# Expert weights in 4 MB loads over two neighbouring slots of a ring

## The reference: what is computed

```
for each block of tokens of expert e:
    gu = xb @ w_gate_up[e] + b_gate_up[e]        # (1024 x 2048) weights, 8 MB
    gate, up = split(gu); gate = min(gate, 7); up = clip(up, -7, 7)
    hmid = (up + 1.0) * (gate * sigmoid(1.702 * gate))
    out = hmid @ w_down[e] + b_down[e]           # (1024 x 1024) weights, 4 MB
y[token] += gate_weight * out
```

## Time and profile before

| what | value |
|---|---|
| time, median of 3 runs | 1261.79 us (1261.73 to 1263.7) |
| span of the profiled execution | 1260.1 us |
| TensorE matmul busy | 1172.9 us (93%) |
| TensorE weight load busy | 505.3 us (40%) |
| VectorE busy | 304.5 us (24%) |
| ScalarE busy | 205.2 us (16%) |
| SyncE's data queue: share of 16 engines | 83.1%, 439.30 MB |

### The profile page before, as it was taken

One profiled execution on the slowest core, in us unless ns is written; L12 is line 12 of the kernel. 1 busy time (PEld: TensorE's weight loads), 2 busy tenths in 40 slices (PEclk: granted clock), 3 DMA queues, 4 the chain that ended last, 5 costly groups with the idle time before them and its releaser, 6 DMA issues.

```text
span 1260.1 us, 17850 instructions
## 1 busy us (share of the span) xinstructions
PE 1172.9 (93%) x6963; PEld 505.3 (40%) x6963; DVE 304.5 (24%) x728; ACT 205.2 (16%) x384; POOL 3.1 (0%) x7
## 2 busy tenths in 40 slices
PE   7999999999899999999999888899999999999895
PEld 3476644685433333333333333333333333333332
DVE  3336463234702111112111111112111112111112
ACT  2120254132201111111111111111111111111111
POOL 0000000000000000000000000000000000000000
PEclk9998899999889999999999999999999999999999
DMA  9710064531889999999999999999999999999993
GB/s 366 322 67 2 2 266 148 219 134 67 347 360 429 426 429 426 428 427 427 428 426 428 428 428 428 427 428 429 427 428 427 429 426 428 427 428 428 428 427 143
DMA packets 37215, 440.48 MB, mean 350 GB/s; under 512 B 5536, under 2 KB 5664, under 8 KB 11456
## 3 DMA queue, kind: packets, MB, share of 16 engines
q1 hardware_dynamic: 36144, 439.30, 83.1%
q10 hardware_dynamic: 1008, 0.21, 0.1%
HBM read 438.45 MB, written 1.05 MB: 349 GB/s over the span
## 4 chain that ended last, share of the span: by engine, by line
PE 64%; DMA 21%; DVE 10%; issue 2%; ACT 2%; DVEq 1%; SPq 0%; ACTq 0%
PE bank L1355 24%; DMA ring<-in_w_gate_up 20%; PE bank L1376 15%; PE bank L1040 4%; PE bank L1070 2%; PE bank L1062 2%; PE bank L1226 2%; PE bank L1217 2%; PE bank L1282 2%; DVE work L914 2%; DVE work L999 2%; DVE work L995 1%; PE bank L1367 1%; DVE work L996 1%; ACT work L580 1%
## 5 line engine op out<-in xcount | busy, mean ns | idle before, releaser
L1355 PE MATMUL bank<-ring,work 128*64 128x512 f32 x2112 | 465.9, 596 | 23.6 <-DMA ring<-in_w_gate_up 23.6
L1355 PEld LDWEIGHTS bank<-ring,work 128*64 128x64 f32 x2112 | 146.8, 137 | 324.3 <-issue 270.8
L1376 PE MATMUL bank<-ring,work 128*64 128x512 f32 x1056 | 233.9, 595 | 22.6 <-ACT work L580 22.6
L1376 PEld LDWEIGHTS bank<-ring,work 128*64 128x64 f32 x1056 | 72.9, 137 | 162.4 <-issue 131.9
L995 DVE TENSOR_SCALAR work<-bank 128x512 f32<-128x512 f32 x33 | 22.8, 692 | 323.1 <-PE bank L1355 323.1
L577 ACT ACTIVATE work<-work 128x512 f32<-128x512 f32 x33 | 20.8, 630 | 472.4 <-DVE work L995 472.4
L909 DVE CAST work<-cst 96x64 bf16 (+1 forms) x34 | 6.5, 191 | 334.7 <-PE bank L1355 334.7
L1336 PE MATMUL bank<-work 64*128 64x512 f32 x272 | 67.6, 615 | 0.7 <-ACT work L586 0.7
L1327 PEld LDWEIGHTS bank<-work 128*128 128x128 bf16 x1632 | 50.6, 99 | 29.1 <-issue 28.3
L1040 PE MATMUL bank<-ring,work 128*128 128x488 f32 x128 | 54.4, 589 | 8.2 <-DMA ring<-in_w_in 8.2
L584 ACT ACTIVATE work<-bank 128x512 f32<-128x512 f32 x33 | 19.7, 597 | 237.2 <-PE bank L1376 237.2
(11 more groups left out here) (232 smaller groups left out, 765.8 us busy)
## 6 DMA issues: line engine op xcount, KB each, us to landing
ring<-in_w_gate_up SPq DMA_DIRECT2D x128, 2048.0 KB, 32.0
ring<-in_w_down SPq DMA_DIRECT2D x64, 2048.0 KB, 31.4
ring<-in_w_mkv SPq DMA_DIRECT2D x8, 1024.0 KB, 23.5
ring<-in_w_in SPq DMA_DIRECT2D x8, 976.0 KB, 17.0
ring<-in_w_o SPq DMA_DIRECT2D x1, 4096.0 KB, 13.1
ring<-in_w_mq SPq DMA_DIRECT2D x1, 4096.0 KB, 24.1
ring<-in_w_mo SPq DMA_DIRECT2D x1, 4096.0 KB, 12.9
work<-in_xT SPq DMA_DIRECT2D x2, 512.0 KB, 8.0
```

Source lines behind the costliest of these rows:

```text
L1355: ins = mm(bank[n // 2][lo:lo + BLK, :], xgT[:, k * BLK:(k + 1) * BLK], up_rows(j, k)[:, n * 512:(n + 1) * 512], start=False, stop=(k == K ...
L1376: ins = mm(bank[3][n * BLK:(n + 1) * BLK, :], lhs, down_rows(j, f)[:, n * 512:(n + 1) * 512], start=(f == 0), stop=(f == KC - 1))
```

## The change

From chunk 10 on, the loads go out in pairs: one transfer of 4 MB fills two neighbouring slots, 32 KB in a row per partition, both in HBM (the arrays are now laid out with two chunks of an expert per partition run) and in SBUF (the seventh and eighth places of `REGION` are swapped, so that each even slot and the next one are neighbours). It waits until the second of the two old chunks has been used for the last time, and both slots' readers wait for the one semaphore of the even slot. The first ten chunks are still loaded one by one, each now as half of a 32 KB run in HBM, and chunks 6 and 7 change places in the order. TensorE still uses and frees chunk by chunk.

```diff
-REGION = (2, 3, 4, 5, 8, 9, 7, 6, 0, 1)
+REGION = (2, 3, 4, 5, 8, 9, 6, 7, 0, 1)
...
+        def slot_pair(j):
+            return ring[:, REGION[j % NSLOT] * SLOT:(REGION[j % NSLOT] + 2) * SLOT]
...
             def load_chunk(j):
                 e, c = divmod(j, NCH)
-                src = wgu[c, :, e, :] if c < NGU else wdn[c - NGU, :, e, :]
-                sp.dma_start(slot(j), src).then_inc(ld_slot[j % NSLOT], 16)
+                src = wgu[c // 2, :, e, :] if c < NGU else wdn[0, :, e, :]
+                sp.dma_start(slot(j), src[:, c % 2 * SLOT:(c % 2 + 1) * SLOT]).then_inc(ld_slot[j % NSLOT], 16)
...
-            load_chunk(6)
+            load_chunk(7)
             sp.wait_ge(S["wm_mm"], 4)
             load_chunk(8)
             load_chunk(9)
             sp.wait_ge(S["rt_mm"], 2)
-            load_chunk(7)
+            load_chunk(6)
...
             def load_next(j, e, lasts):
+
                 c = j % NCH
-                back, freed = (2, c + NCH - NGU) if c < NGU else (1, c - NGU)
+                back, freed = (2, c + 1 + NCH - NGU) if c < NGU else (1, c + 1 - NGU)
                 sp.wait_ge(S["chunks_used"], lasts[2 - back] * NCH + (freed + 1))
-                src = wgu[c, :, bass.ds(e, 1), :] if c < NGU else wdn[c - NGU, :, bass.ds(e, 1), :]
-                sp.dma_start(slot(j), src).then_inc(ld_slot[j % NSLOT], 16)
+                src = wgu[c // 2, :, bass.ds(e, 1), :] if c < NGU else wdn[0, :, bass.ds(e, 1), :]
+                sp.dma_start(slot_pair(j), src).then_inc(ld_slot[j % NSLOT], 16)
...
-            for c in range(NGU, NCH):
-                load_next(NCH + c, 1, (first, first))
+            load_next(NCH + NGU, 1, (first, first))
...
-                    for c in range(NCH):
+                    for c in range(0, NCH, 2):
                         load_next((LEAD + r) * NCH + c, e, lasts)
...
+            def chunk_in(j):
+                if j < NSLOT:
+                    pe.wait_ge(ld_slot[j], 16)
+                else:
+                    pe.wait_ge(ld_slot[j % NSLOT // 2 * 2], (j // NSLOT + 1) * 16)
...
                     if k % ROWS == 0:
-                        pe.wait_ge(ld_slot[(j + k // ROWS) % NSLOT], ((j + k // ROWS) // NSLOT + 1) * 16)
+                        chunk_in(j + k // ROWS)
...
                     if f % (2 * ROWS) == 0:
-                        d = j + NGU + f // (2 * ROWS)
-                        pe.wait_ge(ld_slot[d % NSLOT], (d // NSLOT + 1) * 16)
+                        chunk_in(j + NGU + f // (2 * ROWS))
...
-        "w_router": w_router[0], "b_router": b_router[0], "w_gate_up": by_partition(w_gate_up[0], NGU),
-        "b_gate_up": b_gate_up[0], "w_down": by_partition(w_down[0], NDN), "b_down": b_down[0], "g_final": g_final,
+        "w_router": w_router[0], "b_router": b_router[0], "w_gate_up": by_partition(w_gate_up[0], NGU // 2),
+        "b_gate_up": b_gate_up[0], "w_down": by_partition(w_down[0], NDN // 2), "b_down": b_down[0], "g_final": g_final,
```

## The result

| | before | after |
|---|---|---|
| median | 1262.82 us (1261.73 to 1263.7, 8 runs) | 1265.45 us (1263.86 to 1267.33, 8 runs) |
| span of the profiled execution | 1260.1 us | 1261.9 us |

The ratio is 1.0022, 95% interval 1.0013 to 1.0031: slower by 2.6 us in the medians, between 1.6 and 3.9 us by the interval. Forecast were +1.3 us, 1263.1, and a range of 1257.0 to 1267.8. The profiled execution after, with 1263.86 us, was the fastest of its eight; its span is only 1.8 us above that of before.

The account below looks back on a forecast made before the run. The end was taken as set by the unbroken load stream from chunk 16, plus TensorE's work after the last g3. Start +3.42, tail +3.44, streaming -5.6 gave +1.3 us: 1263.1 us, range 1257.0 to 1267.8.

Parts of the forecast that it names:

- the forecast case: Whole kernel: streaming saves 3 to 9 us and no new gap opens, 1259.7 to 1265.7 us; chance 0.50.
- three signs named for a wrong forecast: Profile after: rate unmoved or moved over 1%, idle DMA engines in a window after 372, or clock below 1.00 after 400.
- rival C: Waits merged into one of 2.4 us lower TensorE's clock; in the last item +2.1 us, 1265.2; chance 0.10.
- D: Load queue runs dry at (20, 21) or the two-item expert: +1 to +3 us, to 1266; chance 0.08.
- Start, +3.4: Start of unbroken stream: pair (16, 17) waits for chunk 17's condition, going out at 371.99 instead of 368.57, +3.4 us.
- Streaming, -5.6: Load stream from (16, 17): 32 KB runs save fixed cost a = 8 ns, 64 ns per pair, 87 pairs, -5.6 us.
- A: Load stream: longer runs save as much again per byte, 11.8 us, net -4.9, 1256.9 us; chance 0.17.
- B: Load stream: 32 KB runs move as two of 16 KB or gain nothing; +6.9, 1268.7 us; chance 0.15.
- The 7.9 us lost on the way: Stream from chunk 16 to last g3: 1222.7 worked out, 1230.56 seen; instruction packets would account for it, carried over unchanged.
- Tail, +3.44: After the last gate-up landing: g2 and g3 land together, so 16 more matmuls follow, +3.44 us.
- No gap at (20, 21): Early stream: pair (20, 21) goes out in time, 393.6 against 394.1, margin 0.5 us, so no gap.
- The expert with two items, 0 with +0.5: Load at the two-item expert: gap of 0.4 us at most, hidden by slower engines; taken as 0, keeping +0.5.

Follow-up runs that it names:

- the run with chunk 16 alone: Changed kernel with only the pair (16, 17) loaded one by one; 1264.05 us, 1.0013 against the kernel before.
- the run of the tail: Changed kernel with only g2 and g3 of the last expert loaded one by one; 1262.52 us, 0.9995 against the kernel before.
- the run with added matmuls in the last two experts: Changed kernel with 8 zero-adding matmul instructions before the wait for g2 in experts 30 and 31; 1264.01 us, 1.0011 against the kernel before.
- long-run experiments: Changed kernel with pairs and waits kept but the old HBM layout, two 16 KB runs per partition; 1270.11 us, 1.0047 against the kernel before.

## Why the prediction was right, and where its sizes were off

The forecast of +1.3 us lies 0.5 below what the profiled execution shows and 1.3 below the medians. The mechanism held, but that the sum came so near is in part luck: the stream gained 0.8 us more than forecast, and 1.2 us more were lost on the way. Of the three signs named for a wrong forecast two came true: a window after 372 shows idle DMA engines (0.04 from 902 to 904), and the granted clock fell below 1.00 after 400. The third did not, as the rate moved by 0.7%. So what happened is the forecast case with a small share of rivals C and D in it.

- **What bounds the kernel**: right. The end follows the unbroken stream of loads from chunk 16 on. The runs that undo the start and the tail move the end by about the amounts worked out (2.8 and 3.4 us, together 5.3, and 6.1 with the last three experts one by one); each of these has an interval of more than 1 us on either side.
- **Start, +3.4**: measured 3.42 in the trace; 2.8 came back when it was undone, with seven pairs (0.5 us) less of the faster stream.
- **Streaming, -5.6**: 87 pairs x 73 ns = -6.4. A run of 32 KB costs 9.713 / 8 = 1214 ns, 9 ns less than two of 611.6; a was 9, not 8. Neither limit (nothing, 11.8 us) came near, so rivals A and B were both wrong. The packets went from 37215 to 24110 [page of either kernel]. Two runs made one in 91 pairs are 91 x 128 packets less, and 91 transfers less are 91 x 16 small ones: 13104 of the 13105. A cut into pieces of 16 KB would not give that.
- **The 7.9 us lost on the way, carried over**: the forecast put them down to packets of instructions. The completions show where they are: the first engine finished the last g3 at 1222.0, as the sum without loss gives (1222.7), the last one at 1230.5. So it is the drift of the engines; that the packets cause it is not shown.
- **Tail, +3.44**: 3.4 measured from the last wait to the end.
- **No gap at (20, 21)**: right, with the margin as small as said: in the run with chunk 16 alone, 3.4 us less of queue opened it.
- **The expert with two items, 0 with +0.5**: the reasoning was that slower engines would hide the gap. They did where the clock stayed (0.0 us at the landing in the run of the tail) and hid all but 0.6 us where it fell. What was missed is that the engines ahead would stand idle in either case. Of the way from 372.14 to the last landing, 372.14 + 2.7 + 87 x 9.713 = 1219.9, 9.1 us are lost instead of 7.9: +1.2, of which 0.6 is seen at the hole; where the other 0.6 went is open.
- **The clock (rival C)**: the term that was mis-sized. The forecast gave it 10% and treated it as a case apart, in the last item only. It is there in every execution with pairs that was profiled, three to six times in each. It costs 1.7 us when it hits the last item and lets through up to 1.1 us of the hole when it hits the item before that. The median (+2.6) stands above the first profile (+1.8), and the runs spread over 3.5 us instead of 2.0. A fall in the last item of some executions would do this, and the run with added matmuls in the last two experts points that way; it is not shown, since the clock of single items is known for profiled executions alone.

Sum for the profiled execution: 3.4 + 0.15 (late from the start) - 6.35 + 1.2 + 3.4 = 1.8 us. The 1.2 is what the other terms leave over, so the sum closes by its making.

How often the last item is hit was not counted; it was in three of the five profiled executions that could show it. Why the tail and the long-run experiments moved the median by a little more or less than their rows is within their intervals.

## What to carry to other kernels

Loads that are made larger are paid for at the two ends of the stream: once where the queue is first short, once behind the last landing, each with one small piece's compute. If only the stream gains, keep small loads at the beginning (until the lead has grown past one piece) and over the last few items, and large ones between: here that turned +2.6 us into -3.3. And look at what a merged wait does to TensorE: the clock stayed after two waits of 1.2 us in every item of two profiled executions, and fell after some two of three waits of 2.2 us or more.

## What the runs showed of the hardware

- The fixed cost of a run per DMA engine is 6.6 to 9 ns from 4 KB to 32 KB (6.6 and 8.5 by the earlier trace rows, 9 by the 9.713 us of a pair). Neither the distance between runs (16 or 32 KB: 1262.25 and 1262.29 us) nor the size of the transfer (2 or 4 MB with runs of 16 KB: 427 and 428 GB/s) changes the rate noticeably.
- In the twelve profiled executions with pairs, 66 waits of TensorE for a pair lasted 2.2 to 2.8 us, amid full work, and 45 of them were followed by 32 matmuls that took 8.5 to 8.8 us instead of 7.09 (3.4 us at 1.2 GHz in the five windows read). So were seven of eight waits of 1.9 to 2.1 us, each right after such an item. After waits for a pair of 1.5 us or less that never happened, nor after the double waits of 1.24 us with single loads. A fall makes TensorE later, so the next wait was mostly one of 0.5 to 0.9 us, and that item was spared.
- The 16 DMA engines drift apart over a stream of 870 us, from 1.5 to 8.5 us between the first and the last completion of a load. A hole lets the last ones catch up (6.3 us before it, 0.4 us behind it), so that several microseconds of idle time for some cost the landing 0.6 us or nothing.
